# First FFN by seven half products per pair, modulation blocks placed beside pairs and in the first retention head

## What is computed

```python
c_act = jax.nn.silu(c)
for i in range(2):
    mod = c_act @ w_ada[i] + b_ada[i]                       # 1024 x 6144
    sh1, sc1, g1, sh2, sc2, g2 = jnp.split(mod, 6, axis=-1)
    h = modulate(rmsnorm(x, norm_mix_g[i]), sh1, sc1)
    m = fourier_mixer(h, ...) if i == 0 else retention_mixer(h, ...)
    x = x + g1[:, None, :] * m
    h = modulate(rmsnorm(x, norm_ffn_g[i]), sh2, sc2)
    gate, up = jnp.split(h @ w_ffn_in[i], 2, axis=-1)       # 1024 x 5632
    x = x + g2[:, None, :] * ((jax.nn.silu(gate) * up) @ w_ffn_out[i])   # 2816 x 1024
shf, scf = jnp.split(c_act @ w_ada_final + b_ada_final, 2, axis=-1)      # 1024 x 2048
return modulate(rmsnorm(x, final_norm_g), shf, scf)
```

## Time and profile before

| | us |
|---|---|
| median of 3 runs | 1628.15 (1628.14 to 1631.49) |
| profiled execution, its own time | 1630.62 |
| its span | 1628.8 |
| PE busy | 1599.9 (98% of the span) |
| DVE busy | 975.2 (60%) |
| ACT busy | 671.1 (41%) |
| POOL busy | 805.4 (49%) |
| HBM traffic over the span | 143 GB/s |

### The profile page before, as it was taken

The page is one execution under the profiler, slowest core; times in us unless marked ns, Lnnn a source line. Parts: engine busy times, 40 slices in busy tenths (PEclk is TensorE's granted clock), DMA queues, the critical chain, the costliest instruction groups (busy, mean ns, idle before and its releaser), DMA issues.

```text
span 1628.8 us, 23557 instructions
## 1 busy us (share of the span) xinstructions
PE 1599.9 (98%) x8190; PEld 1345.3 (83%) x8190; DVE 975.2 (60%) x1599; ACT 671.1 (41%) x1035; POOL 805.4 (49%) x470
## 2 busy tenths in 40 slices
PE   8999998999999999999999999999999999999997
PEld 6785777888888888888888888888888889999996
DVE  6899887878656353442356245171445677777754
ACT  5424444443524322222243423342343456576563
POOL 5899233453344444444452433244243289588562
PEclk9999998999999999999999999999999999999999
DMA  9443266466465565556552322232222233333331
GB/s 382 128 187 91 78 190 242 143 232 233 142 252 188 183 215 196 205 187 213 178 182 79 114 65 79 89 91 89 76 79 67 63 93 115 106 111 113 114 95 62
DMA packets 65465, 234.00 MB, mean 144 GB/s; under 512 B 7264, under 2 KB 7264, under 8 KB 65120
## 3 DMA queue, kind: packets, MB, share of 16 engines
q1 hardware_dynamic: 65376, 232.82, 42.9%
HBM read 230.69 MB, written 2.10 MB: 143 GB/s over the span
## 4 chain that ended last, share of the span: by engine, by line
PE 52%; issue 22%; POOL 16%; DVE 4%; ACT 1%; DMA 1%; POOLq 0%; DVEq 0%; ACTq 0%
PE bank L2014 16%; PE bank L2015 16%; PE bank L2016 16%; POOL w_lo L573 11%; POOL cv_acc L667 2%; DVE mods_ring L1376 1%; PE bank L2048 1%; PE bank L2052 1%; PE bank L2049 1%; DVE f_lo L1400 1%; POOL cv_y L649 1%; POOL diag L661 1%; POOL sq L661 1%; PE ps_stat L2080 1%; DVE x L1418 0%
## 5 line engine op out<-in xcount | busy, mean ns | idle before, releaser
L573 POOL TENSOR_TENSOR w_lo<-w_raw,w_hi 128x1024 fp32r<-128x1024 f32 x208 | 500.5, 2413 | 697.3 <-ACT w_hi L754 685.5
L2014 PE MATMUL bank<-h_hi,w_hi 128*128 128x512 f32 (+1 forms) x1168 | 434.2, 372 | 1.1 <-POOL h_lo L631 0.9
L2016 PE MATMUL bank<-h_hi,w_lo 128*128 128x512 f32 (+1 forms) x1168 | 431.6, 369 | 0.0
L2015 PE MATMUL bank<-h_lo,w_hi 128*128 128x512 f32 (+1 forms) x1168 | 431.2, 369 | 0.0
L754 ACT ACTIVATE w_hi<-w_raw 128x1024 fp32r<-128x1024 f32 x208 | 218.9, 1052 | 192.4 <-PE bank L2016 174.8
L2014 PEld LDWEIGHTS bank<-h_hi,w_hi 128*128 128x128 f32 x1168 | 219.7, 188 | 40.5 <-issue 2.5
L2015 PEld LDWEIGHTS bank<-h_lo,w_hi 128*128 128x128 f32 x1168 | 219.7, 188 | 38.0 <-issue 1.2
L2016 PEld LDWEIGHTS bank<-h_hi,w_lo 128*128 128x128 f32 x1168 | 219.7, 188 | 37.4
L2014 PE MATMUL bank<-f_hi,w_hi 128*128 128x512 f32 (+1 forms) x472 | 174.3, 369 | 0.9 <-DVE z_buf L1920 0.9
L2015 PE MATMUL bank<-f_lo,w_hi 128*128 128x512 f32 (+1 forms) x472 | 174.5, 370 | 0.0
L1376 DVE CUSTOM_DVE_ANT_0 mods_ring<-mods_ring,c_all 128x1024 f32<-128x1024 f32 x144 | 168.5, 1216 | 10.0 <-DMA mods_ring<-w_mods_in 9.0
(11 more groups left out here) (344 smaller groups left out, 2865.2 us busy)
## 6 DMA issues: line engine op xcount, KB each, us to landing
mods_ring<-w_mods_in SPq DMA_DIRECT2D x152, 512.0 KB, 5.9
w_raw<-ff_in_in SPq DMA_DIRECT2D x88, 512.0 KB, 3.6
w_raw<-ret_in SPq DMA_DIRECT2D x64, 512.0 KB, 3.6
w_raw<-ff_out_in SPq DMA_DIRECT2D x32, 512.0 KB, 3.6
w_raw<-cv_ab_in SPq DMA_DIRECT2D x16, 512.0 KB, 6.9
w_raw<-ff_tail_in SPq DMA_DIRECT2D x16, 384.0 KB, 3.1
w_raw<-cv_g_in SPq DMA_DIRECT2D x8, 512.0 KB, 3.9
w_raw<-cv_out_in SPq DMA_DIRECT2D x8, 512.0 KB, 3.6
```

The lines of the kernel that those rows point to most:

```text
L573: pool.tensor_tensor(w_lo[:, s, :], w_raw[:, s, :], w_hi[:, s, :].bitcast(F32), ALU.subtract).then_inc(lo_done, 1)
L2014: pe.matmul(out, w_h, m_h, start=start, stop=False, skip_group_check=onto)
L2015: pe.matmul(out, w_h, m_l, start=False, stop=False, skip_group_check=onto)
L2016: return pe.matmul(out, w_l, m_h, start=False, stop=stop, skip_group_check=onto)
```

## The change

The plain `ffn` is removed on every engine; `last_ffn` becomes `strassen_ffn(layer, ...)`, called for both layers, with the counters of `PAIRS` (now both layers' list, `LP` = 26 pairs each), `z_made`, `ft_lo_done` and others carried on. `c_all` must now live through the pairs, as blocks are summed beside them. So:

- the sums S1, S2 and S4 of a pair share one buffer, `ps_stat` and `ps_bc` by turns: S2 overwrites S1 once its low part is made, S4 overwrites S2; the copy of A21 goes there too. The silu of the gate goes to `bank[1]` (`ps_stat` in a layer's last pair). The sums of h go to `ps_stat` and `ps_bc` and are split in two ops of 512 in place of one of 1024;
- the 72 blocks are placed anew: 21 in the first FFN beside pairs (`PAIR_BLOCKS`: 8 with the groups of sums of h, 13 in the in pairs), 4 in its last part, 31 in retention head 0 (`ring_blocks`), 13 in the last FFN's in pairs, 3 in its last part. A pair block lies in free quarters of `f_hi` and `f_lo`, four pieces of 256 per partition, two places by turns. The ring blocks use `mods_ring` as before;
- head 0 of retention keeps its gates and squares out of `mods_ring` and `c_all` (`gate_of`, `first_sq`, `first_turned`);
- c is spread a third time (`spread_c(2)`, with `c_diagonal` on DVE ahead of the last head's out tiles);
- the norm ahead of the first FFN writes `h_raw`; POOL and ACT do tail unit 3 before the last chunk.

```diff
 # the list, the places of blocks
+PAIRS = [x for layer in range(2) for p, n in enumerate(PARTS)
+         for x in ([("in", layer, p, c) for c in range(1 if p else STD_TILES // 2, n)]
...
+LP = len(PAIRS) // 2
+APART, BY_TILE, BY_PAIR = 22 * SLOTS, (8, 0), 13
+PAIR_BLOCKS = [[first + n for n in range(BY_TILE[layer] + BY_PAIR)] for layer, first in enumerate((APART, 36 * SLOTS))]
+RING_BLOCKS = [*range(PAIR_BLOCKS[0][-1] + 1, 36 * SLOTS), *range(PAIR_BLOCKS[1][-1] + 1, MOD_GROUPS * SLOTS)]
+RING_TAIL = [[(), (), (), range(4)], [(), (), (), range(RING_FIRST[1], len(RING_BLOCKS))]]
+RING_HEAD = [[(), (), (), range(4, 8)], [(), (), (8, 9), (10, 11)], [(12,), (13, 14), (15, 16), (17, 18, 19)],
+             [(20, 21), (22, 23), (24, 25), range(26, RING_FIRST[1])]]
...
-        s3_sum, s1_sum, s2_sum, s4_sum = diag[:], ps_stat[:], ps_bc[:], c_all[:, 0:T]
-        gate_front, gate_back = c_all[:, T:T + H], c_all[:, T + H:2 * T]
+        sums_of = lambda q: (ps_stat, ps_bc)[q % 2]
+        pair_gate = lambda q: ps_stat if q % LP == LP - 1 else bank[1]
+        pair_place = [b[:, 0:8:2, H:T] for b in (over_f_hi, over_f_lo)]
 # SP
+            def ring_block(k):
+                layer, s = int(k >= RING_FIRST[1]), k % SLOTS
+                if k - RING_FIRST[layer] < SLOTS:
+                    sp.wait_ge(half_done, BLOCKS * LP * (layer + 1))
+                else:
+                    sp.wait_ge(msum_step, summed(RING_BLOCKS[k - SLOTS]))
+                sp.dma_start(mods_ring[:, s, :], t["w_mods"][RING_BLOCKS[k]]).then_inc(mods_in[s], 16)
+            def pair_block(layer, n):
+                if n >= len(PAIR_BLOCKS[layer]):
+                    return
+                if n >= 2:
+                    sp.wait_ge(msum_step, summed(PAIR_BLOCKS[layer][n - 2]))
+                src = t["w_mods"][PAIR_BLOCKS[layer][n]].rearrange("p (a n) -> p a n", a=4)
+                sp.dma_start(pair_place[n % 2], src).then_inc(pair_block_in[n % 2], 16)
+            def strassen_ffn(layer, ring):
+                sp.wait_ge(unit_used, U0[name])
+                early = BY_TILE[layer]
+                for n in range(max(early - 2, 2)):
+                    pair_block(layer, n)
+                made = early
+                for q in range(LP * layer, LP * (layer + 1)):
...
+                    if q < LP * layer + 2:
+                        for n in range(2 * (early > 0)):
+                            pair_block(layer, early - 2 + 2 * (q - LP * layer) + n)
+                    elif PAIRS[q - 2][0] == "in":
+                        made += 1
+                        pair_block(layer, made + 1)
...
+            four("qk0", t["ret"], 0, ring=RING_HEAD[0])
+            four("v0", t["ret"], 4, ring=RING_HEAD[1])
+            four("g0", t["ret"], 8, ring=RING_HEAD[2])
+            four("qk1", t["ret"], 16, ring=RING_HEAD[3])
 # POOL
-            tail_chunk_lo(FC - 1)
-            for n in range(3, DC):
+                tail_lo(layer, 3)
+                tail_chunk_lo(first + FC - 1)
+                for n in range(SLOTS, DC):
 # ACT
-                if q:
-                    act.wait_ge(lo_by_vector, 3 * (q - 1) + 1)
+                if q >= 2:
+                    act.wait_ge(lo_by_vector, 3 * (q - 1))
+                if q < LP * layer + 2:
+                    act.wait_ge(ht_lo_done, 2 * DC // 2 * (layer + 1))
                 act.activation(left_raw(q, LEFT_S1), raw_quarter(q, 1, 0), ACT.Copy).then_inc(a21_copied, 1)
 # DVE, left_sum
                     elif i == 2:
-                        v.wait_ge(s_sum, n + 2)
...
-                        v.tensor_tensor(s2, s1, a11, ALU.subtract).then_inc(s_sum, 1)
+                        v.wait_ge(lo_by_vector, 3 * q + 1)
+                        v.tensor_tensor(sums, sums, a11, ALU.subtract).then_inc(s_sum, 1)
                     else:
+                        v.wait_ge(lo_by_vector, 3 * q + 2)
+                        v.tensor_tensor(sums, a12, sums, ALU.subtract).then_inc(s_sum, 1)
 # DVE, groups of sums of h
+                    for n in range(2 * k * (BY_TILE[layer] > 0), min(2 * k + 2, BY_TILE[layer])):
+                        pair_block(layer, n)
 # DVE, before pair 0
-                left_sum(0, 0, 1, 2, 3)
+                left_sum(layer, q0, 0, 1)
                 std_up(2)
-                half_lo(0, LEFT_S1)
-                half_lo(0, LEFT_S2)
+                half_lo(layer, q0, LEFT_S1)
+                left_sum(layer, q0, 2)
+                half_lo(layer, q0, LEFT_S2)
+                left_sum(layer, q0, 3)
                 std_up(3)
 # DVE, an in pair
-                        left_sum(q + 1, 0, 1, 2, 3)
+                        left_sum(layer, q + 1, 0, 1)
+                        pair_block(layer, made)
+                        made += 1
                         half(LEFT_S1)
...
-                        half_lo(q + 1, LEFT_S1)
+                        half_lo(layer, q + 1, LEFT_S1)
+                        left_sum(layer, q + 1, 2)
...
-                        half_lo(q + 1, LEFT_S2)
                         half(LEFT_A22)
                         v.tensor_tensor(c21, bank[2][:, 0:H], u2, ALU.add).then_inc(combined, 1)
+                        half_lo(layer, q + 1, LEFT_S2)
+                        left_sum(layer, q + 1, 3)
 # DVE, head 0
             v.wait_ge(rot_in, 16)
-            rotary(0, 0, 0)
+            ring_blocks(4, 8)
+            rotary(0, 0, 0, range(8, 11))
+            ring_blocks(11, 13)
             rotary(1, 0, 0)
...
-            head_rest(0, 0)
+            head_rest(0, 0, range(13, 16))
+            ring_blocks(16, 26)
...
                 head_gate(h, n)
+                if n == 0:
+                    ring_blocks(26, RING_FIRST[1])
+                    v.wait_ge(msum_step, summed(RING_BLOCKS[RING_FIRST[1] - 1]))
 # DVE and PE, before the last FFN
+            c_diagonal(lambda k: c_2[:, k:k + 1])
             out(f"ro{h}", 4, "n5", per_unit=2)
...
+            spread_c(2)
             stat("n5")
```

More of the change, by code:

```diff
@@ L738, in _ @@
+            for layer, (first, end) in enumerate((("fr_out", "out02"), ("qk0", "out12"))):
+                with pool.Fori(0, (U0[end] - U0[first]) // SLOTS) as i:
+                    for s in range(SLOTS):
+                        lo_part(SLOTS * i + (U0[first] + s), s)
+                strassen_ffn(layer)
             pool.wait_ge(rb_ready, 2)
@@ L1854, in last_ffn, with ring_blocks, rotary @@
                     update(n, BACK, 3, 5)
-                    half_lo(q + 1, LEFT_S4)
-                out("out12", n5, stat)
-            ffn(0, 3, "n4", g)
+                    half_lo(layer, q + 1, LEFT_S4)
+                out(tail(layer), n5, stat, ring=ring)
+            strassen_ffn(0, 3, "n4", [(), ()] + [(k,) for k in range(4)])
             norm(4, ST["n4"])
-            add_bias(SHIFT[4] + 2 * DC, DC)
             SSH = SS0["h1"] - SS0["h0"]
-            def rotary(half, h, n):
+            def ring_blocks(first, end):
+                for k in range(first, end):
+                    ring_block(k)
+            def rotary(half, h, n, ring=()):
                 b0, b1 = bank[2 * half], bank[2 * half + 1]
```

621 lines of the change are left out of this document (300 added, 321 removed).

## The result

| | before | after |
|---|---|---|
| median of the runs, us | 1628.14 (1627.22 to 1631.49, 4 runs) | 1605.44 (1602.31 to 1605.89, 4 runs) |
| profiled execution, span, us | 1628.8 | 1603.5 (time 1605.29) |
| ahead of the first FFN, us | 489.66 | 488.13 |
| first FFN | 366.60 | 336.96 |
| retention | 426.24 | 432.88 |

The ratio of the times is 0.9853, with a 95% interval of 0.9834 to 0.9871: faster by 1.5%, inside the forecast range, but 5.2 us above the forecast time. The two profiled spans differ by 25.3 us; 23.8 of them lie in the three edited stages and 1.5 ahead of them. The part ahead of the first FFN is not edited; it took 489.66 us in the one trace of the kernel before and 484.35 to 488.13 over all runs with the change, so I compare stages, not spans.

The account below looks back on a forecast made before the run. TensorE (PE), busy 98% of the span, was taken to bound the kernel. Terms -30.5 - 0.9 + 1.5 + 1.7 + 0.3 = -27.9 us off the median 1628.15 gave 1600.2 us, range 1596.9 to 1608.

Parts of the forecast that it names:

- Rival 1: Start of the first FFN slips further, as DVE has no idle left: 6 us in place of 1.5, 1604.7; chance 0.12.
- Rival 2: Pairs lose their rhythm between ScalarE and DVE: 26 pairs lose 0.5 us each, +13, 1613; chance 0.10.
- the products' other bound: First FFN's gain counted by product rows instead of by whole stages: 29.8 us less.
- Products: First FFN: 26 pairs by seven half products take work off PE, -30.5 us from the two stages' lengths.
- Tail: Both FFNs' tails: POOL makes tail unit 3's low part before the last chunk's, ending a PE wait; -0.9 us, bounds -0.9 and 0.
- Blocks in pairs: 26 in pairs of both FFNs carry a modulation block at 0 us, DVE busy 8.4 of 9.76 us.
- The chain argument: In pairs: S1, S2, S4 share one buffer; S4 ends 2.1 us into the next pair, PE wants it 8.4 in.
- Start of the first FFN: Eight tiles before pair 0: 8 blocks on DVE and late landings delay PE, +1.5 us, bounds 0 and 6.
- Pass of c: After the last projection, ahead of the statistics: c_2 is spread again on PE, unhidden, +1.7 us, bounds 1.2 and 1.8.
- First retention head: 31 blocks go where DVE idles; late rotaries and next head's weights mostly covered, +0.3 us, bounds 0 and 3.
- Sum: All terms together: -27.9 us off the median 1628.15, giving 1600.2 us.
- Rival 3: Pairs' weights come late behind blocks on SP's queue; at 1.5 us late per pair +11, 1639; chance 0.03.

## Why the prediction was right and wrong

The sign and the large term came out as worked out, and the time, 1605.44 us, lies in the range. But it lies above the forecast's own band of 1597.9 to 1603, in the part of the range that was kept for rivals 1 and 2, and neither of these came: that the range held it is luck in part. (The band's upper end is loosely added: the products' other bound and 1.5 us more give 1602.4, with 1.5 in each of the two stages 1603.9. The result is above both.)

- **Products, -30.5.** Right. The last FFN's length was the right measure: the first takes 335.38 us when nothing else is late, 31.2 below its 366.60; the 0.7 beyond is the tail's.
- **Tail, -0.9.** Right in kind, undersized and outside its bounds: no wait at either tail after, and putting the old order back costs 0.78 and 0.74 us, 1.5 together. The step took the bracket of 0.47 for the cost; by starts it is 0.75.
- **Blocks in pairs, 0.** Right. Pairs are 9.76 and 9.71 us, DVE busy 8.1 to 8.8 (8.4 forecast). The chain argument held too, and its margin is now known.
- **Start of the first FFN, +1.5, bounds 0 and 6.** Right in place: the product of tile 7 on DVE is the last wait. In size it is 1.6 in the profiled execution, 0.9 in the next, 0 where block 7 lands in time. So the 0.8 us put on DVE's work did not show by itself, and the landing, put at 0.7, goes with all of it; that the sum fits the first execution is luck. Rival 1 (6 us) did not come.
- **Pass of c, +1.7.** Right: 1.74 to 1.78 us on the path.
- **First retention head, +0.3, bounds 0 and 3.** This is the step that failed. Measured: 5.2 us in the first profiled execution against the run with three blocks in the gating, 3.5 for the wait and 1.7 at half the clock; 6.8 in the second. The text had the nine blocks end 1 to 4 us after the next rotary could start (it was 3.74) and found cover in PE's next two tiles. That cover is for the first rotary's banks. PE wanted the second rotary's, behind the subtractions and a reciprocal of 3.35 us, with 3.2 us of slack, and this place was not followed. It also named the late weights of the next head and costed them by when PE uses them; their price was on ACT and POOL, where they arrived together, and from there on DVE, 3.0 us. Neither delay alone cost more than a wait of 0.46 (the rotary late: 0.46; the subtraction held: 0). And it priced no clock behind a wait.
- **Sum.** -31.2 (with the first tail) + 1.6 + 1.8 + 5.2 - 0.3 (the later wait of retention that got shorter) and -0.8 for the last FFN give -23.7, against the -23.8 of the three stages (1128.97 to 1105.20).

Rival 2 had no cause here: with a block alone the pairs keep 9.76 us, with 1.4 us more on DVE they don't. Rival 3 had its mechanism, weights behind blocks on SP, right in the wrong place: not beside the pairs, where nothing waited, but in the retention head, and it took back 5 us, not the gain.

## What to carry to other kernels

Where work is put into an engine's idle time, follow each engine that it delays (here SP's queue, POOL's burst, DVE's order) to the same later deadline, and add the delays up against the one slack they share; each alone looked free. The slack is to be read at the last thing in line that another engine waits for, not at the first. Price the time at half the clock behind a wait of PE too: behind waits of 1.90 to 3.63 us it cost 1.6 to 3.0 us here, behind waits up to 1.16 none. And count a wait by the distance of starts, not by its bracket.

## What the runs showed that was not expected

- TensorE behind pauses. Before each wait of 1.90 us and more it had been busy for 60 us without a gap, at 2.4 GHz. Behind a pause of 1.90 us it ran at 1.2 GHz from the fifth product on, for about as long as behind 3.33 (1.7 us lost in each); behind 3.63 us in the changed kernel's second run for 14 products (3.0 lost); behind 0.46, 0.91 and 1.16 us not for any whole product. Of the eight waits of 1.90 us and more, seven lost 1.6 to 1.8 us and one 3.0: the loss does not follow the length of the wait. The Trainium skill (TensorE: Matmul & The Clock Gate, Part 1) has the lower clock as the state that activity releases; the trace agrees, as each time some 7 to 14 products ran slowly and those behind them at full speed.
- A subtraction of two SBUF tiles took 2.885 us on DVE beside POOL's unbroken splits, where the shortest of its kind took 0.687. The Trainium skill (SBUF — State Buffer, Who interferes with whom) has such an op contend with a GpSimd op that reads SBUF; the trace agrees. When POOL had a break at that moment, it took 0.69 again. Whether the two meet was set here by when the weights were asked for.
